# Values products of both attentions, from one 128-query product to two 64-query products in the array's column halves

## What is computed

```
# stick-breaking attention, strictly causal (s < t)
z = einsum('bhqd,bhkd->bhqk', q_i, k) * scale
log_fail = where(mask, log_sigmoid(-z), 0.0)
suffix = cumsum(log_fail, axis=3, reverse=True) - log_fail
a = where(mask, exp(log_sigmoid(z) + suffix), 0.0)
return einsum('bhqk,bhkd->bhqd', a, v)

# latent attention, causal (s <= t)
s = (einsum('bqhd,bkhd->bhqk', qn, k_nope) + einsum('bqhr,bkr->bhqk', qp, k_pe)) * scale
p = softmax(where(key_idx <= q_idx, s, min), axis=-1)
return einsum('bhqk,bkhd->bqhd', p, v)
```

## Time and profile before

| what | value |
|---|---|
| median of 3 runs | 2938.91 us (2938.07 to 2939.73) |
| the profiled execution, its own time | 2935.31 us |
| its span (first to last instruction) | 2933.5 us |
| PE busy | 2758.5 us, 94% of the span |
| DVE, ACT, POOL busy | 47%, 23%, 32% |
| granted TensorE clock | 0.98 of full speed over the span |

### The profile page before, as it was taken

One profiled execution on the slowest core, in us unless ns is written; L12 is line 12 of the kernel. 1 busy time (PEld: TensorE's weight loads), 2 busy tenths in 40 slices (PEclk: granted clock), 3 DMA queues, 4 the chain that ended last, 5 costly groups with the idle time before them and its releaser, 6 DMA issues. The chain is left out here.

```text
span 2933.5 us, 48563 instructions
## 1 busy us (share of the span) xinstructions
PE 2758.5 (94%) x20356; PEld 2195.1 (75%) x20356; DVE 1374.6 (47%) x1332; ACT 682.8 (23%) x966; POOL 945.1 (32%) x417
## 2 busy tenths in 40 slices
PE   7999999999999999999998989989999999998886
PEld 6777778887888888888876767776767767676675
DVE  7844441124532122212565643345457465564589
ACT  3433330011211001000233234441222121222321
POOL 4222214443444444444533211103111121213365
PEclk9999999999999999999999999999999999998998
DMA  3100001112111111111121100001011111112343
GB/s 124 36 29 29 29 15 50 50 44 107 43 50 49 45 50 50 46 47 50 57 79 65 65 22 14 14 29 59 31 42 34 49 38 42 34 42 95 115 151 107
DMA packets 40746, 156.11 MB, mean 53 GB/s; under 512 B 4640, under 2 KB 5152, under 8 KB 39200
## 3 DMA queue, kind: packets, MB, share of 16 engines
q1 hardware_dynamic: 31392, 110.21, 11.4%
q10 hardware_dynamic: 9216, 43.78, 4.0%
HBM read 133.00 MB, written 20.97 MB: 52 GB/s over the span
## 5 line engine op out<-in xcount | busy, mean ns | idle before, releaser
L2376 POOL TENSOR_TENSOR w_hi<-w_raw,one 128x1024 fp32r<-128x1024 f32 x199 | 389.8, 1959 | 1931.9 <-PE dps L283 1500.4
L283 PE MATMUL dps<-h_hi,w_hi 128*128 128x512 f32 x1904 | 608.3, 395 | 46.0 <-issue 11.1
L283 PE MATMUL dps<-h_lo,w_hi 128*128 128x512 f32 x1904 | 602.2, 392 | 0.0
L283 PE MATMUL dps<-h_hi,w_lo 128*128 128x512 f32 x1904 | 600.2, 391 | 0.0
L2378 POOL TENSOR_TENSOR w_lo<-w_raw,w_hi 128x1024 fp32r<-128x1024 f32 x199 | 527.5, 2651 | 15.6
L283 PEld LDWEIGHTS dps<-h_hi,w_hi 128*128 128x128 f32 x1904 | 358.4, 190 | 134.8 <-issue 40.3
L283 PEld LDWEIGHTS dps<-h_lo,w_hi 128*128 128x128 f32 x1904 | 360.8, 190 | 75.8 <-issue 0.2
L283 PEld LDWEIGHTS dps<-h_hi,w_lo 128*128 128x128 f32 x1904 | 360.5, 189 | 76.1
L300 PE MATMUL dps<-h_hi,w_hi 128*128 128x512 f32 x352 | 128.8, 426 | 5.3 <-DVE rw_t L1891 5.3
L300 PE MATMUL dps<-h_lo,w_hi 128*128 128x512 f32 x352 | 129.5, 430 | 2.5 <-DVE rw_t L1891 1.6
L300 PE MATMUL dps<-h_hi,w_lo 128*128 128x512 f32 x352 | 121.7, 412 | 1.6 <-DVE rw_t L1891 1.6
(11 more groups left out here) (355 smaller groups left out, 4218.7 us busy)
## 6 DMA issues: line engine op xcount, KB each, us to landing
w_raw<-w_stream SPq DMA_DIRECT2D x200, 512.0 KB, 3.3
x_again<-x_t ACTq DMA_DIRECT2D x2, 4096.0 KB, 13.0
gates<-gate_out ACTq DMA_DIRECT2D x16, 512.0 KB, 2.9
tmp<-gates ACTq DMA_DIRECT2D x16, 512.0 KB, 4.3
x_t<-x_res ACTq DMA_DIRECT2D x4, 1024.0 KB, 3.9
out_t<-x_again SPq DMA_DIRECT2D x16, 256.0 KB, 2.0
back<-branches ACTq DMA_DIRECT2D x7, 512.0 KB, 8.9
x_res<-x_t ACTq DMA_DIRECT2D x2, 1536.0 KB, 12.1
```

The costliest lines, as they stand in the source:

```text
L283: mm = k.nc.tensor.matmul(k.dps[0:rows, pair, h * HALF:(h + 1) * HALF], w[:, slot, sub + t, 0:rows], x(t)[:, h * HALF:(h + 1) * HALF], sta ...
L2376: g.tensor_tensor(k.w_hi[:, s], k.w_raw[:, s], ones, ALU.mult).then_inc(k.sem("w_hi_done"), 1)
```

## The change

Each values product is issued as two products, one for each half of the block's 128 queries: the stationary operand is 128 keys x 64 queries, the same 64 columns of values stream, and the result goes to partitions 0 to 63 or 64 to 127 of the same place in PSUM. `HEADS` is the pair of slices (0 to 64, 64 to 128). Nothing else changes; every other line moves down by one or two.

```diff
@@ values() of the stick-breaking attention
         for t in range(n):
-            mm = mul(sb_sums(k, h)[:, b * HD:(b + 1) * HD], k.sb_at[:, g % 2, t * P:(t + 1) * P],
-                     k.sb_v[:, first + t, h * HD:(h + 1) * HD], start=g in (0, HEAD_END[0] + 1) and t == 0,
-                     stop=first + t == b, skip_group_check=True)
+            for n_q, queries in enumerate(HEADS):
+                mm = mul(sb_sums(k, h)[queries, b * HD:(b + 1) * HD], k.sb_at[:, g % 2, t * P + n_q * HD:t * P + (n_q + 1) * HD],
+                         k.sb_v[:, first + t, h * HD:(h + 1) * HD], start=g in (0, HEAD_END[0] + 1) and t == 0,
+                         stop=first + t == b, skip_group_check=True)
         mm.then_inc(k.sem("sb_pv_done"), 1)
@@ values() of the latent attention
             for t in range(n):
-                mm = mul(k.dps[:, 1, HALF + b * HD:HALF + (b + 1) * HD], k.mla_pt[:, g % 2, t * P:(t + 1) * P],
-                         k.mla_v[:, h, first + t, :], start=g == 0 and t == 0, stop=first + t == b, skip_group_check=True)
+                for n_q, queries in enumerate(HEADS):
+                    mm = mul(k.dps[queries, 1, HALF + b * HD:HALF + (b + 1) * HD], k.mla_pt[:, g % 2, t * P + n_q * HD:t * P + (n_q + 1) * HD],
+                             k.mla_v[:, h, first + t, :], start=g == 0 and t == 0, stop=first + t == b, skip_group_check=True)
             mm.then_inc(k.sem("mla_pv_done"), 1)
```

## The result

| what | before | after |
|---|---|---|
| median (5 runs each, side by side) | 2938.91 us (2937.75 to 2943.17) | 2922.06 us (2921.48 to 2925.02) |
| the profiled execution, its own time | 2935.31 us | 2921.65 us |
| its span | 2933.5 us | 2919.1 us |

The changed kernel is faster by 16.85 us: the ratio is 0.9943, with a 95% interval from 0.9929 to 0.9958. The prediction was 2930.2 us, a gain of 8.7 us, with a range from 2906 to 2946. The sign and the range hold, and so does the mechanism that was priced, halves side by side with a drain around each group; the gain is about twice as large. Part of the surplus is a mis-sized term in the attentions, part comes from a stage far behind them that the prediction never looked at.

A forecast was written before the change was run, and what follows sets the result against it. TensorE, busy 94% of the span, was taken to bound the kernel, and weight loads its values groups. Stick-breaking -6.4 and latent -2.3 us made -8.7: a median of 2930.2 us from 2938.9, range 2906 to 2946.

The forecast's parts named there:

- halves side by side with a drain around each group: Likeliest case for the values products in both attentions: 2930.2 us, own range 2920 to 2938, chance 0.70.
- Loads side by side, a step of 0.058 us: Values products: column halves load and multiply together, two steps a product, 0.117 us in place of 0.223.
- The rival of serial loads: Values products: the halves' loads take turns because they share all rows, 0.117 us a step; 2980 us, chance 0.12.
- A drain on both sides, of the size in the earlier trace: Around each values group: first load 0.20 us later going in, next load 0.07 before the last matmul's end coming out.
- all four lengths: Values groups of 4, 3, 2, 1, first load to next other load: 0.62, 0.50, 0.38, 0.27 us.
- No drain: Rival: changing columns alone drains nothing, a group of 4 takes 0.47 us; -32 us in all, 2907 us, chance 0.11.
- a longer drain: Rival: column halves take 0.1 us more on each side of a group; +19 us, 2949 us, chance 0.07.
- The small groups hide under waits: Small values groups ahead of TensorE's waits grow at no cost; uncovered, about +1.3 us a stick-breaking pair.
- The stick-breaking sum, -6.4: Stick-breaking attention: 24 values groups a pair, mostly gains of groups that waited; -1.6 us a pair, -6.4 for four.
- the column "ahead of a turn" of the table: Load-to-load change for values groups followed by a turn: n 4 -0.02, 3 +0.08, 2 +0.19, 1 +0.30 us.
- The latent sum, -2.3: Latent attention: values groups sum to -0.29 us a head, -2.3 for eight heads.
- what is saved between waits stays saved: Both attentions: ACT and DVE have slack, idle 15 and 10 us of a pair's 42.5, so TensorE's savings last.

The follow-up runs named there:

- one half first: Changed kernel with each group's products reordered: all blocks for queries 0 to 63, then all for 64 to 127; 2944.33 us, ratio 1.002 against before.
- the third block left whole: Changed kernel with the third block of each group of 4 as one whole product, the other three halved; 2950.49 us, ratio 1.0037 against before.
- quarters: Changed kernel with each product issued as four of 32 queries instead of two of 64; 2932.67 us, ratio 0.9984 against before.
- the order set by hand: One GpSimd wait added in the gated merge: w_lo waits for VectorE's add of the same tile; before with it 2933.26 us, changed kernel with it 2924.91.
- this mildest trace of before: First of three profiles of the unchanged kernel before, the one shown in the result: 2935.31 us for the profiled execution.
- the second: Second of three profiles of the kernel before, nothing changed; the two repeat runs took 2936.79 and 2940.88 us.
- the fours-only kernel: Changed kernel with only groups of 4 key blocks halved, groups of 1 to 3 whole as before, in both attentions; 2923.29 us, ratio 0.995 against before.

## Why the prediction was right, and where its sizes were off

**Loads side by side, a step of 0.058 us: right.** The trace of after shows it, and so do all kernels with alternating halves. The Trainium skill ("TensorE: Matmul & The Clock Gate", Part 3: Packing small matmuls, The mechanism) would have the loads wait, since the halves share their rows; the trace doesn't agree: 0.117 us for two halves of two loads and two matmuls each. The rival of serial loads is out. The kernel with one half first shows what its price would have been like: 25 us more than after in the two attentions, with part of the overlap still there.

**A drain on both sides, of the size in the earlier trace rows: right**, to 0.01 us in all four lengths, and 0.14 us a change by the third block left whole. No drain and a longer drain are out.

**The small groups hide under waits: right.** In the stick-breaking attention, halves or wholes for them make almost no difference (281.5 and 281.4 us, with the lower clock of one first pair in it); in the latent one they cost 1.6 us, predicted with (0.10 + 0.14 + 0.03) x 8 = 2.2.

**The stick-breaking sum, -6.4 against -8.6: the step that failed is the column "ahead of a turn" of the table.** It was measured from load to load. But before the change the turn's load runs ahead and then lies unused until its matmul can go, as it did at the group's start. By the matmuls, the gain is the same whoever follows. TensorE rows of a group of 4 between two turns, before:

```profile
301.39 0.60 PE L603 MATMUL dps<-const,sb_a 128*128 128x128 f32 x4
...
302.67 0.61 PE L603 MATMUL dps<-const,sb_a 128*128 128x128 f32 x4
```

and after:

```profile
295.89 0.60 PE L603 MATMUL dps<-const,sb_a 128*128 128x128 f32 x4
...
297.03 0.66 PE L603 MATMUL dps<-const,sb_a 128*128 128x128 f32 x4
```

From the end of one turn to that of the next it is 1.29 us before (301.99 to 303.28) and 1.20 after (296.49 to 297.69): -0.09, or -0.08 from unrounded times, where the table has -0.02. For a group of 4 ahead of scores it is -0.08 (predicted -0.07), for 3 +0.02 with either follower (predicted +0.08 and +0.03), for 2 +0.13 (predicted +0.19 and +0.14). Windows of the second pair and of the projections behind it, before:

```profile
195.00:235.40 40.40, 38.20 (x263) 30.82 (x262) 30.88 (x28) 26.68 (x48) 0.00 (x0) 1.00 0.04 13
235.40:278.20 42.80, 40.67 (x187) 32.70 (x188) 11.79 (x12) 7.00 (x13) 17.11 (x8) 1.00 0.12 39
```

Against after (above) the pair is 2.3 us shorter and the stretch behind it 0.3 longer: 2.0 for 1.6. Followed group by group through the third pair, to the end of what follows each on TensorE, the seven groups that wait for nothing gain 0.25 us together (predicted 0.03), the seven that wait 1.76 (predicted 1.60, with the smaller groups ahead of them priced too high), and the last ones 0.08 (predicted a loss of 0.04): 2.1 for 1.6. From first to last values product the first pair is 2.6 us shorter (40.7 to 38.1), with 1.3 us less of the lower granted clock, and each other pair 2.2; the three stretches between the pairs are 0.2 us longer each. That is the 8.6.

**The latent sum, -2.3 against -4.0.** By groups it is -0.30 a head, -2.4 for eight, where -2.3 was predicted. The rest is one place: the stretch behind one head's last values group, before and then after:

```profile
1802.20:1820.40 18.20, 16.43 (x74) 12.64 (x73) 3.66 (x9) 5.18 (x11) 5.40 (x3) 0.91 0.17 53
```

```profile
1793.10:1809.80 16.70, 14.93 (x74) 11.73 (x72) 3.61 (x9) 5.12 (x10) 5.65 (x3) 1.00 0.10 31
```

The same 74 matmuls take 18.2 us at a granted clock of 0.91 and 16.7 at 1.00. Before, the granted clock falls to its lower level (1.2 in place of 2.4 GHz) for 3.4 us about 1817, behind a wait of 2.0 us for ACT's exponential. That wait isn't enough: after has it too, 2.01 us ahead of the same load at 1807.64, and the clock doesn't fall there. All traces with the latent attention as before have 10.2 us of that level in it, the four with its products as in after 6.8; quarters has 13.7. So this part of the gain, which the sum has no term for, repeats, and why the stretch keeps the clock in the one and not in the other is not shown.

**Not foreseen: the last stretch.** The prediction said that what is saved between waits stays saved, and looked no further than the attentions. In the merge, far behind them, the order of two engines at one shared resource turned: 88.7 to 93.3 us before, 82.9 after (windows over its eight adds). 5.8 us of the 14.4 between the two profiles are from there (88.7 to 82.9). Not all of it is the order: with the order set by hand the kernel before still takes 85.5 us, with 4.5 us at the lower granted clock against 1.8 in after. So the order accounts for 3.2 of the 5.8 against this mildest trace of before, and for 7.8 of 10.4 against the second. 1.9 us go back in front of the merge (33.8 to 35.7 us) and 1.4 in the recurrent stage. The prediction's list of what would go wrong had only waits in the attentions. Why an earlier end of the attentions turns the order is open: the fours-only kernel keeps before's order (a merge of 93.1 us) although its latent attention ends as early as after's (1959.3 and 1960.5 us).

**What of the number is luck.** With the order set in both kernels the change is worth 8.4 us, and 8.7 were predicted. The agreement is chance: it is 11.7 us in the attentions, where 8.7 were priced, less what unedited stages took back.

## What to carry to other kernels

Where a product is bound by its weight loads and uses the array whole with few columns streaming, two column halves that alternate instruction by instruction about halve the time of a product (0.117 us in place of 0.223 here). The price is a drain at each change of shape. Here it paid for groups of four products, most of all where the array had emptied anyway; three about broke even (+0.02), and two lost (+0.13) where no wait hid them. Price such an edit by the ends of matmuls, not by the starts of loads that run ahead. And before a difference is put down to the edit, compare the stages that weren't edited, and profile the kernel before more than once: here 5.8 of 14.4 us came from a stage some 750 us behind the last edited instruction, over half of it because two engines met in another order there.

## What the runs showed of the hardware

- Two 128 x 64 column halves with fp32 operands load and multiply side by side although they share all rows: 0.058 us a step, the four of a product 0.117, against 0.223 for one 128 x 128 product. Four 128 x 32 quarters are no faster (0.056 us a step).
- With eight loads for one half ahead of the eight for the other, the other half began 0.29 us behind, and the sixteen loads took 0.83 us in place of 0.55.
- A change of the columns in use costs about 0.14 us (third block whole); the first load comes 0.07 us before the recorded end of the last matmul.
- An add on VectorE with both inputs in SBUF and a subtraction or multiplication on GpSimd don't overlap, and the one that starts second is recorded as longer: the add's 1.23 us become up to 3.4 (before, at 2762.80), the subtraction's 2.4 become 3.25 to 3.5.
- With 878 matmuls in a loop's body in place of 590 TensorE stood 3.7 us at the loop's turns, and its granted clock fell behind that; the cause was not tried.
